# Compression rows of the sample caches: one page a transfer over 128 partitions, and four half-height copies a turn in place of one

## The reference, cut to what matters

```python
def compress(rows, pos, w1, b1, w2):
    B, T = rows.shape[:2]
    c = rows.reshape(B, T // CMP_STRIDE, CMP_STRIDE, NSA_KV, HEAD_DIM)
    blocks = jnp.concatenate([c[:, :-1], c[:, 1:]], axis=2) + pos[None, None, :, None, :]
    n_cmp = blocks.shape[1]
    flat = blocks.transpose(0, 1, 3, 2, 4).reshape(B, n_cmp, NSA_KV, CMP_LEN * HEAD_DIM)
    return jax.nn.gelu(flat @ w1 + b1) @ w2

nsa_past = cache_nsa_kv[l, page_table].reshape(n_dec, past, 4, NSA_KV, HEAD_DIM)
kc = compress(rows[:, :, 0], pos[0], w1[0], b1[0], w2[0])
vc = compress(rows[:, :, 1], pos[1], w1[1], b1[1], w2[1])
```

## Time and profile before

| | |
|---|---|
| median of 3 runs | 1976.57 us (1974.04 to 1982.81) |
| the profiled execution | 1972.21 us, span 1970.5 us |
| PE, PEld busy | 1805.3 us (92%), 1589.8 us (81%) |
| DVE, ACT, POOL busy | 987.4, 740.8, 506.8 us |
| the phase `front` | ends at 178.5 us, 9% of the span |
| DMA | 229.30 MB in 169903 packets, 45018 of them under 512 B |
| mean granted clock of PE | 0.977 |

### The profile page before, as it was taken

The page is one execution under the profiler, slowest core; times in us unless marked ns, Lnnn a source line. Parts: engine busy times, 40 slices in busy tenths (PEclk is TensorE's granted clock), DMA queues, the critical chain, the costliest instruction groups (busy, mean ns, idle before and its releaser), DMA issues. The chain is left out here.

```text
span 1970.5 us, 31185 instructions
## 1 busy us (share of the span) xinstructions
PE 1805.3 (92%) x11465; PEld 1589.8 (81%) x11465; DVE 987.4 (50%) x1911; ACT 740.8 (38%) x1477; POOL 506.8 (26%) x604
## 2 busy tenths in 40 slices
PE   4999999998876799999997998999999999999996
PEld 4888777997643588878886887999999999976784
DVE  4233331333333677777777642333333333365997
ACT  3234411312321377777777332111111111243453
POOL 5020032422453442222211101121111222123523
PEclk9899999999998899999998998999999999999998
DMA  8534343356987993333312121111111111164643
GB/s 188 82 100 156 118 160 116 120 178 205 322 244 248 194 225 65 65 67 73 75 56 78 65 89 40 45 52 53 43 43 43 43 52 44 46 233 149 201 136 142
DMA packets 169903, 229.30 MB, mean 116 GB/s; under 512 B 45018, under 2 KB 113477, under 8 KB 169665
## 3 DMA queue, kind: packets, MB, share of 16 engines
q1 hardware_dynamic: 143298, 152.77, 26.5%
q0 software_dynamic: 24400, 72.81, 13.5%
q10 hardware_dynamic: 2080, 2.10, 0.4%
HBM read 192.65 MB, written 40.24 MB: 118 GB/s over the span
## 5 line engine op out<-in xcount | busy, mean ns | idle before, releaser
L121 PE MATMUL gate_acc<-o_T_hi,w_gate_split_hi 128*128 128x352 f32 x528 | 171.3, 324 | 2.3 <-ACTq L2818 2.3
L121 PE MATMUL up_acc<-o_T_hi,w_up_split_hi 128*128 128x352 f32 x528 | 171.3, 324 | 0.7 <-DVEq L2882 0.7
L122 PE MATMUL gate_acc<-o_T_lo,w_gate_split_hi 128*128 128x352 f32 x528 | 170.1, 322 | 0.0
L123 PE MATMUL gate_acc<-o_T_hi,w_gate_split_lo 128*128 128x352 f32 x528 | 169.9, 322 | 0.0
L122 PE MATMUL up_acc<-o_T_lo,w_up_split_hi 128*128 128x352 f32 x528 | 169.9, 322 | 0.0
L123 PE MATMUL up_acc<-o_T_hi,w_up_split_lo 128*128 128x352 f32 x528 | 169.8, 322 | 0.0
L2306 ACT ACTIVATE pa_scores<-pa_scores,pa_neg_max 128x128 f32<-128x128 f32 (+1 forms) x192 | 143.4, 747 | 15.6 <-DVE pa_neg_max L2346 12.2
L2394 DVE TENSOR_TENSOR pa_probs_T_lo<-pa_t,pa_probs_T_hi 128x512 fp32r<-128x512 f32 (+2 forms) x240 | 123.9, 533 | 29.0 <-ACT pa_probs_T_hi L2321 26.7
L2940 POOL TENSOR_TENSOR w_gate_split_lo<-w_gate,w_gate_split_hi 128x1024 fp32r<-128x1024 f32 x21 | 50.4, 2401 | 340.5 <-ACT w_gate_split_hi L2828 340.5
L2321 ACT ACTIVATE pa_probs_T_hi<-pa_t 128x512 fp32r<-128x512 f32 (+2 forms) x240 | 110.9, 477 | 67.2 <-PE pa_t L2245 64.2
L2245 PE MATMUL pa_t<-ident,pa_scores 128*128 128x128 f32 x688 | 115.4, 274 | 20.4 <-DVE pa_probs_T_lo L2394 20.4
(11 more groups left out here) (456 smaller groups left out, 4722.8 us busy)
## 6 DMA issues: line engine op xcount, KB each, us to landing
w_down_raw<-in_w_down SPq DMA_DIRECT2D x59, 512.0 KB, 4.6
fox_k_pages<-in_cache_fox_kv SPq DMA_DIRECT2D x64, 256.0 KB, 7.2
w_rows<-in_cache_fox_kv POOLq DMA_DIRECT2D x48, 256.0 KB, 8.5
w_gate<-in_w_gu SPq DMA_DIRECT2D x22, 512.0 KB, 3.9
w_up<-in_w_gu SPq DMA_DIRECT2D x22, 512.0 KB, 3.9
w_rows<-in_w_in SPq DMA_DIRECT2D x5, 2048.0 KB, 8.4
sel_pages<-in_cache_nsa_kv POOLq DMA_DIRECT2D x64, 128.0 KB, 8.1
pa_k_fox<-scratch_kf_d POOLq DMA_DIRECT2D x32, 256.0 KB, 6.9
```

What stands on the lines that cost most here:

```text
L121: pe.matmul(out, a[0][at], b[0][bt], start=start, stop=False)
L122: pe.matmul(out, a[0][at], b[1][bt], start=False, stop=False)
L123: return pe.matmul(out, a[1][at], b[0][bt], start=False, stop=stop)
```

## The change

A page is loaded by one transfer of 128 KB: 128 partitions, one token each, in one run of 1 KB at both ends. A sequence's half is four transfers, not eight. The transposes then put (g, e) on the partitions and tokens along the columns, so even and odd tokens stand side by side in PSUM, and the copies part them: for each g and r a piece of 64 partitions and 256 values, from partitions 64g.. of PSUM (every second element) to partitions 64r.. of SBUF. ACT and DVE run four such instructions a turn in place of one. The transposes are as many as before, of the same size. Matmuls are untouched.

```diff
-        rows = [ph.far(f"cmp_rows{i}", [P, 4, 4, 2, HD]) for i in range(SB)]
+        rows = [ph.far(f"cmp_rows{i}", [P, PAGES, 4 * HD]) for i in range(SB)]
...
             for i in range(4):
-                p = 4 * part + i
-                side = slice((p % 2) * 64, (p % 2) * 64 + 64)
-                src = d["cache_nsa_kv"][0, ds(pages[i], 1)].rearrange("a (n r) w g e -> (a n) r (w g) e", r=2)
-                for r in range(2):
-                    eng.dma_start(rows[q % SB][side, p // 2, :, r, :], src[:, r, 0:4, :]).then_inc(s_rows[part][q % SB], 16)
+                src = d["cache_nsa_kv"][0, ds(pages[i], 1)].rearrange("a n w g e -> (a n) (w g e)")
+                eng.dma_start(rows[q % SB][:, 4 * part + i, :], src[:, 0:4 * HD]).then_inc(s_rows[part][q % SB], 16)
...
-                for g in range(G):
-                    for a in range(2):
-                        at = g * 256 + a * P
-                        part = rows[q % SB][:, 2 * half + a, 2 * k + g, :, :].rearrange("p r e -> p (r e)")
-                        ins = pe.transpose(tr[n % 2][:, at:at + P], part, c.ident[:, :])
+                for j in range(4):
+                    ins = pe.transpose(tr[n % 2][:, j * P:(j + 1) * P], rows[q % SB][:, 4 * half + j, k * P:(k + 1) * P], c.ident[:, :])
...
+        def pieces(t):
+
+            b, k, s, half = t
+            for g in range(G):
+                for r in range(2):
+                    at = np.s_[r * HD:(r + 1) * HD, s, g, :, 32 * half:32 * half + 32]
+                    hi, lo = (tile[at].rearrange("p f n -> p n f") for tile in xt[k])
+                    yield hi, lo, tr[number[t] % 2][g * HD:(g + 1) * HD, :].rearrange("p (n f r) -> p r n f", f=8, r=2)[:, r, :, :]
...
-                act.activation(kept(xt[k][0], s, half), turned(n), ACT.Copy).then_inc(s_hi, 1)
+                for hi, lo, src in pieces(t):
+                    ins = act.activation(hi, src, ACT.Copy)
+                ins.then_inc(s_hi, 1)
...
-                dve.tensor_tensor(kept(xt[k][1], s, half), turned(n), kept(xt[k][0], s, half), ALU.subtract).then_inc(s_lo, 1)
+                for hi, lo, src in pieces(t):
+                    ins = dve.tensor_tensor(lo, src, hi, ALU.subtract)
+                ins.then_inc(s_lo, 1)
```

More of the change, by code:

```diff
@@ L331, in turn @@
                 if k == 0 and half == 0:
-                    pe.wait_ge(s_rows[0][q % SB], 128 * (q // SB + 1))
-                    pe.wait_ge(s_rows[1][q % SB], 128 * (q // SB + 1))
+                    pe.wait_ge(s_rows[0][q % SB], 64 * (q // SB + 1))
+                    pe.wait_ge(s_rows[1][q % SB], 64 * (q // SB + 1))
                 if n >= 2:
                     pe.wait_ge(s_lo, n - 1)
-                for g in range(G):
-                    for a in range(2):
-                        at = g * 256 + a * P
-                        part = rows[q % SB][:, 2 * half + a, 2 * k + g, :, :].rearrange("p r e -> p (r e)")
-                        ins = pe.transpose(tr[n % 2][:, at:at + P], part, c.ident[:, :])
+                for j in range(4):
+                    ins = pe.transpose(tr[n % 2][:, j * P:(j + 1) * P], rows[q % SB][:, 4 * half + j, k * P:(k + 1) * P], c.ident[:, :])
                 ins.then_inc(s_tr, 1)
```

## The result

The changed kernel takes 1998.63 us (median of 6, 1995.68 to 2003.84), the kernel before 1976.80 beside it: ratio 1.0108, interval 1.0083 to 1.0132. Slower by 1.1%, where the prediction had 1983.6 and at most 1992. The execution profiled took 1999.34 us (span 1997.3); the one profiled of before lay 4.4 us under its median, so the two profiled executions lie 27.1 us apart where the medians lie 21.8.

The account below looks back on a forecast made before the run. The prediction took PE, 92% busy, as the bound, so only the end of `front` counts. Its terms 0.4 + 1.9 + 1.7 + 0.4 + 7.6 - 5.2 = +6.8, taken as +7 us, gave 1983.6 us, range 1971 to 1992.

Parts of the forecast that it names:

- The bound, the loads: Up to step 0: only the end of `front` counts; rows load at the weights' pace, 324 against 184 GB/s.
- The price of a turn's copies: Four pieces a turn cost 2.43 us on ACT and 2.40 on DVE, against 1.12 and 1.11 before.
- the dear bound: Upper price of a turn's copies: 622 ns a piece with stride, 2.49 us a turn.
- the slope of 28: End of `front`: 28 us for each us of a turn's price.
- Step 1: Before step 0: copies eat the 7 us the loads gain; step 0 at 30.5 against 30.19, +0.4 us.
- weights late: Rival at the start: ACT's rounding of weight piece 1 ends at 20, not 17.12; +10 us, chance 0.12.
- Step 2: Steps 0, 1 and positions: 0.2 at turn 6, 0.4 low clock, 1.3 wait for DVE's positions; +1.9 us.
- Step 3: Steps 2 and 3, 256 columns: turns 12 and 13 wait 0.4 and 1.3, +1.7 us; low clock +0.4 more.
- Step 4: Steps 4 to 9: third turns wait, +2.0 us; 1.85 before each of steps 6, 8, 10, +5.6; together +7.6.
- Step 5: Later in `front`: row waits of 1.48 and 2.05 us and 1.7 of low clock near 120 go; -5.2 us.
- Three rivals: Late weight piece 1, +10 us (0.12); three more low-clock stretches, +12 (0.15); pieces at 2.7 us a turn, +15 (0.08).

Follow-up runs that it names:

- loads_alone: Changed kernel with the copies of before, one instruction a turn on ACT and DVE, even and odd tokens not parted: 1970.3 us, 0.9953 of the kernel before.
- pieces_alone: Kernel before, its loads and transposes kept, with four copy pieces a turn on ACT and DVE: 1999.8 us, 1.0107 of the kernel before.
- after_gate0: Changed kernel with the loads of sequence 1's rows waiting for piece 0 of the weights: 1992.7 us, 1.0073 of the kernel before.
- after_runs: Changed kernel with each piece's two loops swapped, writing contiguous runs and reading PSUM with a stride: 1972.5 us, 0.9965 of the kernel before.
- after_again: Changed kernel unaltered, measured and profiled a second time: 1994.7 us, 1.0083 of the kernel before.
- runs_gate0: Changed kernel with pieces written in contiguous runs and sequence 1's row loads waiting for weight piece 0: 1972.1 us, 0.9965 of the kernel before.

## Why the prediction failed, step by step

What failed is the price of a turn's copies and the start, and with them the low clock; the path, a turn through PE, ACT and DVE over two buffers, was right.

**The bound, the loads.** Right: most of the loss is there at the end of `front` (21 of the 26.8 us between the profiles), rows load like weights (350 against 184 GB/s), and copies, not loads, end the first stretch. "The 7 us that the loads gain are eaten" is what `loads_alone` and `pieces_alone` show.

**The price of a turn's copies**: mis-sized. Taken 2.43 and 2.40, bounds 1.66 and 2.49; measured 2.60 (5.20 to 5.25 for two turns on ACT) and 2.58 (5.15 for two on DVE), above the dear bound. The nearest rows, the prompt's pieces, were 6 to 7% too cheap. They do not have the same strides, as the prediction says: they write 64 values apart (256 bytes), these 66 apart (264), and they write plain numbers, these rounded ones. Which of the two makes the difference no run here shows; along the row rounding costs nothing (598 ns below, 597 for plain numbers at L1600). The forecast worked its dear bound out for DVE alone (622 a piece, measured 630) and used it for both engines. ACT's rows in the same trace, over all of the span by form, gave it too:

```profile
L2321 ACT ACTIVATE pa_probs_T_hi<-pa_t 128x512 fp32r<-128x512 f32 x120 | 71.8, 598 | 31.8 <-PE pa_t L2245 29.7
L2321 ACT ACTIVATE pa_probs_T_hi<-pa_t 128x256 fp32r<-128x256 f32 x40 | 15.3, 383 | 23.2 <-PE pa_t L2245 23.2
```

The stride costs 1121 - 598 = 523 ns for 512 values; half of that on 383 is 645 ns a piece, where 643 were measured. 0.17 us (2.60 for 2.43, 2.58 for 2.40, on average 0.175) by the slope of 28 is **4.9 us**.

**Step 1, the start**: +0.4 forecast, +3.6 found. ACT's rounding was taken to end at 17.12 as before; it ended at 19.5 (the rival "weights late" with 2.4 of its 2.9 us). That the weights have "most of their bytes" by 8 us was the wrong argument: ACT waits for the whole piece. Holding back the rows of sequence 1 gives **2.0 us** (`after_gate0`). Of the 1.2 left, 0.9 are dearer copies (two turns on ACT and three on DVE stand one behind the other before step 0) and 0.3 are weights still later than forecast (ACT's pieces begin at 17.43 there).

**Step 2, positions**: +1.9 forecast, +2.6 found; PE's wait for `cmp_pos_split` was 1.24 us where 1.3 stood. The forecast speaks of the low clock in steps 1 and 2, but the granted clock reads 1.00 there, until 30.19 and from there to 46.09; that four transposes take 1.05 us at 31.61 and 0.60 at 34.88 in the kernel before stays without a cause here.

**Step 3, steps 2 and 3**: +2.1 forecast, +5.7 found. PE's waits are 3.2 where 1.7 stood. The rest is low clock: the stretch is 17.1 us long instead of 13.6, and as everything comes later it now covers the eight products of the wide tables, 6.4 us instead of 4.0. Its length does not go with the pieces' price: 13.6 us in `pieces_alone`, 17.1 in `after_runs`.

**Step 4, steps 4 to 9**: +7.6 of waits forecast, 9.8 found in `after_again` (6.1 before steps 6, 8 and 10, 3.8 in six third turns, where 5.6 and 2.0 stood). All three places were right, each by 2.0 against 1.85.

**Step 5, given back**: of -5.2, the waits of 1.48 and 2.05 did go. The 1.7 us of low clock did not: there is none at 120.0 any more, but one at 99.9 (97.9 in `after_again`), and that one does not need the new waits, since `loads_alone` and `after_runs` have it too.

So the forecast's +6.8 lacks 4.9 us of price, 2.0 of weights and, of low clock, some 4 us in `after_again` (PE's busy time over that of before: 1.5 more in the wide tables where 0.4 stood, 1.3 more in steps 4 to 9 where 1.7 less stood) and 7.8 in the first profile (1.9, 4.4, and 1.5 behind step 10). That makes 17.8 and 21.5 at the end of `front`, where 18.8 and 21.0 were found, so 1 us of the first stays without a place. The 4.9 us are taken from a slope; counted where they stand, PE's extra waits are 0.9 at the start, 1.5 in steps 2 and 3 and 2.2 in steps 4 to 9, 4.6 in all. Three rivals, priced one at a time at +10, +12 and +15 and each held unlikely, came in part together. The forecast treated them as alternatives, and they need not be: the dear price does not keep the weights from coming late, and the two stretches at 151.1 and 178.4 were seen with dear pieces only. How much of the low clock belongs to the change, and how much to the one execution, stays open.

**The best version.** `after_runs` beats both kernels: 0.9965, and 2 us short of `loads_alone`, which parts nothing (their intervals overlap). With the wait of `runs_gate0` its step 0 comes 1.9 us earlier in the profile, with the same median.

## What to carry to other kernels

When a transfer is made faster by moving a rearrangement into the copies behind it, price the copies first, in their new form, and walk one tile through all engines that touch it: over the two buffers here it was the sum of their prices that set the pace (27.5 us for each us), not the busier engine. Work the price out for each engine from its own rows. Let a copy out of PSUM take the stride where it reads and run along the row where it writes; here that alone turned +1.0% into -0.35%. And what is loaded faster can make its neighbours late: here holding back what is needed later started the products 2 us earlier in the profile, and holding it back until the neighbour had landed made it late itself. The medians show no gain from it.

## What the runs showed of the hardware

- A strided write costs ScalarE and VectorE the same for each element, whatever they cost without it. From 512 and 256 elements: along the row (601 and 381 ns) ACT needs 0.86 ns an element and DVE (692 and 423) 1.05; at 264 bytes a step (1121 and 643, 1107 and 630) both need 1.87. Left over as fixed price of one instruction are 153 to 165 ns in all four. The shapes are 128x512 and 64x256; the number of partitions costs nothing in the one pair at hand (ACT, 256 values along the row: 383 ns on 128 partitions, 381 on 64).
- A stride on the PSUM side was free in the same rows: ACT 601 and 381 ns against 598 and 383 without any, DVE 692 against 691.
- The Trainium skill, SBUF — State Buffer, section "Door 1: The DMA port swizzle", says that an access which leaves its 16-byte line pays a penalty; the rows agree for writes, with 0.8 to 1.0 ns. The forecast had this price in its rows of before and did not ask whether the copy could do without it.
- The same program, with the same waits of 2.0 us before steps 6, 8 and 10 to 0.01 us, was granted 34.1 us of low clock before 215 us in one execution and 20.5 in the other.
